# Moving the reload of the residual rows from the end of the weights' queue to the eighth expert's turn

## The reference

```python
for e in range(N_EXPERTS):                     # 32
    gate, up = jnp.split(t @ w_gate_up[e], 2, axis=-1)     # 1024 x 1024 per expert
    y = (jax.nn.silu(gate) * up) @ w_down[e]               # 512 x 1024 per expert
    out = out + combine[:, e:e + 1] * y.astype(jnp.float32)
...
x = x + hierarchical_moe(rms_norm(x, ffn_norm[l]), ...)
return rms_norm(x, final_norm)
```

## Time and profile before

| | us |
|---|---|
| median of 3 runs (1338.07 to 1338.4) | 1338.19 |
| time of the profiled execution | 1337.05 |
| its span, first to last instruction | 1334.9 |
| TensorE busy | 1283.0 (96%) |
| VectorE busy | 628.7 (47%) |
| ScalarE busy | 395.7 (30%) |
| GpSimd busy | 372.9 (28%) |
| DMA, mean over the span | 218 GB/s |

### The profile page before, as it was taken

How to read it: one execution, slowest core, us unless ns; L and a number is a source line. 1 busy time by engine, 2 the same in 40 slices (tenths; PEclk the granted TensorE clock), 3 DMA queues, 4 the chain that set the end, 5 groups by cost and what they waited for, 6 DMA issues and landing times. The chain is left out here.

```text
span 1334.9 us, 18654 instructions
## 1 busy us (share of the span) xinstructions
PE 1283.0 (96%) x6804; PEld 807.0 (60%) x6804; DVE 628.7 (47%) x1050; ACT 395.7 (30%) x955; POOL 372.9 (28%) x417
## 2 busy tenths in 40 slices
PE   7999999899989999999999999999999999999996
PEld 6788889788869888995445555333333333333332
DVE  3324888788868888863122223622122122122225
ACT  4023636264435445441111123111111111111113
POOL 2256645466454746120100000710000000000002
PEclk9999999999999999999999999899999999999999
DMA  6793212122121212433226533499999999999996
GB/s 211 243 336 99 80 34 79 33 80 64 48 63 49 64 52 66 120 97 116 78 64 240 216 126 116 189 395 415 425 424 425 425 428 427 425 424 426 426 423 257
DMA packets 130854, 290.63 MB, mean 218 GB/s; under 512 B 6420, under 2 KB 109049, under 8 KB 112733
## 3 DMA queue, kind: packets, MB, share of 16 engines
q1 hardware_dynamic: 125168, 277.89, 54.8%
q0 software_dynamic: 3552, 8.20, 1.6%
q10 hardware_dynamic: 2061, 3.50, 0.8%
HBM read 269.32 MB, written 24.12 MB: 220 GB/s over the span
## 5 line engine op out<-in xcount | busy, mean ns | idle before, releaser
L2049 DVE TENSOR_SCALAR ee<-ee 128x256 f32<-128x256 f32 x32 | 10.5, 330 | 333.6 <-ACT ee L1936 333.6
L2028 POOL DMA_INDIRECT expert_out<-yy,row_at x30 | 29.4, 980 | 391.7 <-ACT yy L1922 391.7
L707 PE MATMUL bank<-h_sums,ring 128*128 128x256 f32 x384 | 91.1, 380 | 0.0
L707 PEld LDWEIGHTS bank<-h_sums,ring 128*128 128x128 f32 x384 | 71.9, 190 | 9.2
L707 PE MATMUL bank<-h_mix,weights_0lo 128*128 128x256 f32 x256 | 60.5, 390 | 6.8 <-issue 5.5
L1727 PE MATMUL bank<-x_rows,select 128*64 128x512 bf16 x416 | 62.8, 382 | 0.0
L707 PE MATMUL bank<-h_sums,weights_0hi 128*128 128x256 f32 x256 | 60.5, 379 | 0.0
L1323 PE MATMUL bank<-x_rows,ring 128*128 128x512 f32 x128 | 56.9, 607 | 3.1 <-PEq L467 3.1
L707 PEld LDWEIGHTS bank<-h_mix,weights_0lo 128*128 128x128 f32 x256 | 48.8, 195 | 17.3 <-issue 10.9
L717 PE MATMUL bank<-weights_0lo,h_mix 128*128 128x128 f32 x512 | 58.8, 276 | 0.0
L1323 PE MATMUL bank<-weights_2down,ring 128*128 128x512 f32 x128 | 57.1, 597 | 1.7 <-DVE weights_2down L1525 1.7
(11 more groups left out here) (378 smaller groups left out, 2625.0 us busy)
## 6 DMA issues: line engine op xcount, KB each, us to landing
weights_0lo<-in_w_gate_up SPq DMA_DIRECT2D x11, 2048.0 KB, 17.1
weights_0hi<-in_w_gate_up SPq DMA_DIRECT2D x11, 2048.0 KB, 21.5
weights_0down<-in_w_down SPq DMA_DIRECT2D x11, 2048.0 KB, 21.2
weights_1down<-in_w_down SPq DMA_DIRECT2D x11, 2048.0 KB, 22.2
weights_1lo<-in_w_gate_up SPq DMA_DIRECT2D x11, 2048.0 KB, 17.9
weights_1hi<-in_w_gate_up SPq DMA_DIRECT2D x11, 2048.0 KB, 22.3
weights_2lo<-in_w_gate_up SPq DMA_DIRECT2D x10, 2048.0 KB, 17.5
ring<-in_w_gate_up SPq DMA_DIRECT2D x10, 2048.0 KB, 21.9
```

The lines of the kernel that those rows point to most:

```text
L707: mm = pe.matmul(bank[:, 0:HALF_T], w[:, k], h[:, k], start=(fresh and k == 0), stop=(k == HALF_K - 1), skip_group_check=True)
L2028: pool.indirect_dma_start(out=half_rows, out_offset=bass.IndirectOffsetOnAxis(ap=row_at[:, e:e + 1], axis=0), in_=yy[e % 2][:], in_offset= ...
L2049: st.link(dve.tensor_scalar(ee[q][:], ee[q][:], BIG, 1.0, ALU.min, ALU.add))
```

## The change

The load of `x_home` and its two waits move from behind the turns into turn 7 of SyncE (`FIRST - 1`), behind that turn's three loads of weights. Nothing else is changed.

```diff
@@ sync_main
                     if not (isinstance(e, int) and (e < 1 or e - 1 >= NE - WB)):
                         sp.wait_ge(dn_mm, e)
                         load_down(sp, g, e - 1 + WB, (w - 1) % WB)
+                    if isinstance(e, int) and e == FIRST - 1:
+                        sp.wait_ge(gathered, EARLY)
+                        sp.wait_ge(split, 4 * SPLITS)
+                        sp.dma_start(h_rows[:], g["x_home"]).then_inc(x_again, 16)
                 over_experts(sp, turn)
-                sp.wait_ge(gathered, EARLY)
-                sp.wait_ge(split, 4 * SPLITS)
-                sp.dma_start(h_rows[:], g["x_home"]).then_inc(x_again, 16)
                 last["final_gain"](sp)
```

## The result

| | before | after |
|---|---|---|
| median of 11 runs each, taken together, us | 1337.31 | 1341.34 |
| lowest to highest, us | 1336.16 to 1339.20 | 1337.58 to 1344.13 |
| ratio, 95% interval | | 1.0025 [1.0016, 1.0035] |
| profiled execution, us | 1337.05 | 1339.05 |
| its span, us | 1334.9 | 1336.9 |

The change makes the kernel slower, by 3.3 us as the ratio has it (2.1 to 4.7). The profiled execution is one of the quickest of the eleven after (only one is quicker), and in it the forecast of +2.0 us on the span came out exactly. It will turn out that this is partly luck, and that the median is the better witness.

What follows compares the result with a forecast made beforehand. TensorE was taken as the bound with loads hidden, the finish as bound by GpSimd's gathers. A 4.9 us delay less 3.0 slack gave +2.0 us: 1339.1 profiled, plus 1.1 for the median, 1340.2 us; range 1338.6 to 1342.2.

Steps and rivals of the forecast that it cites:

- (1): SyncE's full queue: x takes one slot, so each of the 64 weight loads behind it lands 4.95 us later.
- (2): TensorE's lead hides the shift until expert 30: its second gate and up half costs +1.7 us, its down matrix +4.9 in all.
- (3): Expert 31's down load beside the gathers loses 0.4 us (0 to 0.95); the last matmuls start 4.9 us later.
- (4): Finish gathers start 1.7 us later, the second at 1304.0; VectorE's sums end at 1324.9; x's absence gives nothing.
- rival (b): First gathers land sooner without x, the second after 7.71 us, not 10.75: 1336.9 us, at best 1335.2; chance 0.04.
- (5): Finish: late rows move by 4.9 us, 3.0 of it slack; VectorE's first root starts at 1325.2, +2.0 us.
- Rival (a): TensorE's clock falls in the new waits near the end, costing 1.7 to 3.4 us: 1341.9 to 1343.6 us; chance 0.20.
- Rival (c): DMA engines have spare rate the queue doesn't use, x fits in, time stays 1338.2 us; chance 0.08.

Runs made afterwards that it cites:

- h2: Kernel after, unchanged, in a second set of runs with its own trace: 1342.46 us, ratio 1.0039 to the kernel before.
- g2: Kernel after plus two idle matmuls in TensorE's wait ahead of expert 31's down matmuls: 1340.17 us, ratio 1.0019 to the kernel before.
- e1: Kernel after with x not read back at all and the residual left out of the result: 1334.78 us, ratio 0.9981 to the kernel before.
- e3: Kernel after with x loaded in turn 7 and once more in turn 26: 1345.48 us, ratio 1.0058 to the kernel before.
- h1: Kernel before with only the final norm's gain loaded late, once two tiles are summed: 1336.05 us, ratio 0.9990 to the kernel before.
- i1: Kernel before with only the final norm's gain loaded late, in a repeated set of runs: 1336.44 us, ratio 0.9989 to the kernel before.
- h3: Kernel after with one tile of x in turn 7, three at the end, and the gain late: 1336.16 us, ratio 0.9992 to the kernel before.
- e4: Kernel after with half of x in turn 7, half behind the last weights: 1339.23 us, ratio 1.0008 to the kernel before.
- g3: Kernel before with a semaphore for each gather of a pair, VectorE's sums reordered to match: 1338.38 us, ratio 1.0009 to the kernel before.

## Why the prediction was right where it was, and wrong where it was not

The direction, the mechanism and the place were right; the time, 1341.34, lies in the range, but it is 1.1 us above the forecast. Beside its own kernel before, the ratio of 1.0025 stands against a forecast of 1.0015, which its interval just leaves out. By its middle value it is the case "slower by more than 0.2%", to which I gave 0.28, though the interval reaches down to 0.16%.

(1) *The shift of a slot: right.* From the base, expert 30's down matrix landed 4.3 us later in the first trace; over three traces of it (446.5, 446.9, 447.3) the mean is 446.9, against 442.0 over six with x at the end: 4.9 us, where the step had 4.95. The load issued at 1257 us lands after 36.0, 36.5 and 36.8 us, where I had 36.6.

(2) *Where the cover ends: right within a turn.* In the first trace the first wait is for the second half of expert 30's gate and up matrix, as said; in h2 there is one of 0.7 us before it, for expert 29's. The matmuls on expert 30's half start 1.1 us later from the base than before (426.19 against 425.11), not 1.7, because the half landed at 426.15, 0.6 us sooner than the 1283.95 - 857.17 = 426.78 of the forecast; in h2 they start 1.5 us later.

(3) *The loss beside the gathers: the step that failed in size.* "I take 0.4", with 0.95 as the upper bound. Between the two last landings there are 6.4 us in all three traces, where it was 4.8 to 5.0: the loss is 1.4 to 1.5 us, beyond my bound. The reason I gave, that most of the load passes before the gathers start, did not hold even in my own times: the second gather was to be issued at 1304.0, and the slot of the load was to run from 1304.25 to 1309.25, all of it beside the gathers. And the gathers did not start 1.7 us later: in the first trace the second was issued at 1301.84 - 856.66 = 445.18 from the base, and before at 1302.32 - 857.17 = 445.15 (0.5 us later in h2, 0.9 in g2). That the load loses 0.5 us more than x lost in that place (5.9 us for x) no run explains. With it the last matmuls start 5.4, 5.8 and 6.2 us later from the base in after, h2 and g2, where I had 4.9, and less the 3.0 us of slack that makes 2.4, 2.8 and 3.2 in place of 2.0. The profiled execution agreed with my times to 0.1 us because it had begun the experts 0.5 us sooner and its loads were the earliest of the three: that was luck.

(4) *The gathers: wrong in their start and in what makes them long, without effect on the sum.* The store of expert 29's rows was issued 1.2 us later from the base, as the step has it in kind, but the first gather followed it after 7.3 us in place of 8.5, so that the gathers started as before; why the store was quicker no run shows. In rival (b) I wrote that "x is not what makes them long". e1 refutes this: 10.7 becomes 7.0 us when x is not there at all. I read the median over four gathers as proof against x because the last of them is issued when x has almost landed; a gather that lands late may well hold up those behind it, and that row could not tell. What the change itself gives them is another matter: there "this gives nothing" held nearly, as the engines do carry as many bytes as before. The first sum comes at 455.2, 455.7 and 456.2 us from the base in after, h2 and g2, against 456.0, not 1.7 later. The root is what VectorE waits for, 3 us and more behind the sums, so it doesn't show in the time. Rival (b) needed a real gain for the gathers and an absent shift; the change brought at most 0.8 us of the first, and the shift arrived whole.

(5) *The finish: right.* 1314.69, 1321.63 and 1325.23 for 1314.7, 1321.7 and 1325.2, and the bound changed over to ScalarE's root as said. The shift of 4.9 us that this step took over from (3) was 5.4 us from the base, and the root's 2.0 was 2.5.

*Rival (a), the clock: real, and I gave it too little.* With a stretch at 1.2 GHz on expert 31's down matmuls it costs 1.7 us, the cheaper half of what I had priced, in four of six traces with a wait like that, h2 (the same kernel as after) among them. I had argued that the waits lie between bursts and that a stretch before 1305 would be spent in waiting; but it falls on the down matmuls themselves, at 1311.7. The Trainium skill ("TensorE: Matmul & The Clock Gate", Part 1) has the clock follow how busy the engine was. The traces agree in kind: it fell behind waits of 1.8 us and more, in four of six, and never there behind 1.3 us; that the same 2.33 us did it in h2 and not in the first trace, nothing here explains. So it is no rival but a part of the case: about +2.8 us from the loads, and 1.7 more in some executions, together 3 to 5, with which the two sets of runs are in keeping (ratios 1.0025 and 1.0039). How often it falls was not counted beyond these traces, so its share in the medians stays open. So does the scatter: in the first set the kernel after spreads over 6.6 us against 3.0, but the kernel before itself spreads over 6.5 us in the 21 runs beside h2, so a wider scatter is not shown.

*Rival (c), the shift absorbed: false.* The weights landed 4.9 us later, and e3's second slot arrived whole as well.

## What to carry to other kernels

In a queue that is worked off in order and never runs dry, an early place for a load is not free: it delays every load behind it by its slot, and the place to pay is where the lead of the engine that consumes them has run out. The load that nobody waits for may still cost at its late place, through what shares the DMA engines with it; but moved ahead in the same full queue it only hands its place to another load. What helped here was to hold a load back until the gathers were through, for which it must not be needed yet (the gain, held back by one wait). Compare single traces from a common event behind the parts that vary, and price the clock whenever a change turns an uninterrupted engine into one that waits 2 us at a time.

## What was not expected of the hardware

- Indirect gathers issued by GpSimd took 10.7 us beside 2.6 MB of other loads (x and the gain), 8.8 and 9.4 us without the 0.5 MB of the gain (h1, i1), 7.0 us without the 2.1 MB of x (e1).
- The clock fell behind waits of 1.82 us (h3), 1.83 (e4) and 2.33 us (h2), though TensorE had been busy for 379.3 of the 380 us from 900 to 1280 us in h2, at a granted clock of 1.00; behind waits of 1.27 us there it never did (six traces), and behind the same 2.33 us in the first trace of after it did not.
- Where a queue is far behind, the issue of some loads holds SyncE: 0.43 us before, 2.19 us for the same load after (landing 35.5 and 39.8 us after issue), and up to 5.57 us in e3, where loads landed 40 to 45 us after issue. It isn't a function of that time alone: expert 30's down matrix, with 39.4 us to landing after, held it for 0.38 us. No cost of it is seen here; a load held up at its issue would have stood in the queue in any case. The timeline of SyncE in e3:

```profile
1244.07 2.83 SPq L1653 DMA_DIRECT2D weights_0lo<-in_w_gate_up  x1
1246.95 4.24 SPq L1653 DMA_DIRECT2D weights_0hi<-in_w_gate_up  x1
...
1265.18 5.57 SPq L1653 DMA_DIRECT2D weights_0down<-in_w_down  x1
```

- The profile seems to give two DMAs on one semaphore landing times that are not their own: with a shared semaphore the first gather of the first pair is shown with 8.4 us, with one of its own (g3) with 10.0 us. That the shared semaphore is the reason is inferred, from two executions. So the times of `ring` and `weights_2lo` are compared above only between kernels of the same form.
